# Attention heads of two transformer blocks taken in pairs, two gates by tanh instead of sigmoid, and one weight unit moved

## The reference, cut to what matters

```
first block:   ada = silu(c) @ w_ada + b_ada          # six vectors of 1024: shift, scale, gate, twice
               h = modulate(rmsnorm(x), ...);  proj = h @ w_in
               o_gla  = rmsnorm(gated linear attention, 4 heads) * silu(gr)
               o_moba = causal softmax attention, 8 heads of 64, with a relative bias
               x += gate_a * (concat(o_gla, o_moba) @ w_out)
               h = modulate(rmsnorm(x), shift_m, scale_m)
               x += gate_m * (relu(h @ w_ff1)**2 @ w_ff2)          # d_ff = 4096
second block:  z = rmsnorm(x) @ w_in_2
               attention of 8 heads of 64: softmax(q k^T / 8 + log(number of patterns that see the pair)) v
               conv = silu(layer_norm(depthwise convolution of 31 taps of a * sigmoid(b)))
               x += concat(attn, conv) @ w_out_2
               16 experts of width 2816, each takes its 32 best tokens: (silu(t w1) * (t w3)) w2
```

## Time and profile before

| | us |
|---|---|
| median of three timed runs | 1866.55 |
| the profiled execution | 1867.52 |
| its span, first to last instruction | 1865.8 |
| TensorE busy, share of the span | 1368.2, 73% |
| VectorE busy | 271.8, 15% |
| ScalarE busy | 230.3, 12% |
| GpSimd busy | 39.3, 2% |
| mean granted TensorE clock | 0.832 of full speed |
| data read from memory | 647.38 MB, 348 GB/s over the span |

### The profile page before, as it was taken

One profiled execution on the slowest core, in us unless ns is written; L12 is line 12 of the kernel. 1 busy time (PEld: TensorE's weight loads), 2 busy tenths in 40 slices (PEclk: granted clock), 3 DMA queues, 4 the chain that ended last, 5 costly groups with the idle time before them and its releaser, 6 DMA issues.

```text
span 1865.8 us, 24015 instructions
## 1 busy us (share of the span) xinstructions
PE 1368.2 (73%) x10574; PEld 839.2 (45%) x10574; DVE 271.8 (15%) x557; ACT 230.3 (12%) x530; POOL 39.3 (2%) x64
## 2 busy tenths in 40 slices
PE   7997999999999686565656747666665766756665
PEld 4584888888656343232323414233231423423232
DVE  1213200005952201010000100001010000100001
ACT  1333222002133110000100000010000100000010
POOL 0000000002020000000000000000000000000000
PEclk9998999999989777787777777777787787777778
DMA  9736343432442999999999999999999999999998
GB/s 348 304 125 270 154 172 125 181 137 110 183 187 92 380 438 432 432 433 424 440 430 433 429 431 429 429 435 433 432 433 431 435 433 433 433 433 433 422 441 342
DMA packets 48248, 649.02 MB, mean 348 GB/s; under 512 B 3832, under 2 KB 6336, under 8 KB 31056
## 3 DMA queue, kind: packets, MB, share of 16 engines
q1 hardware_dynamic: 45152, 643.90, 81.7%
q10 hardware_dynamic: 2848, 3.55, 0.6%
q0 software_dynamic: 208, 1.00, 0.1%
HBM read 647.38 MB, written 1.06 MB: 348 GB/s over the span
## 4 chain that ended last, share of the span: by engine, by line
DMA 58%; PE 12%; DVE 1%; issue 1%; ACT 0%; POOL 0%; SPq 0%; DVEq 0%; PEldq 0%; ACTq 0%; POOLq 0%
DMA ring<-in_w 58%; PE ps L1185 11%; DVE small L1083 0%; DVE arena L1133 0%; DVE arena L1135 0%; DVE arena L1079 0%; DVE xT L1177 0%; ACT L701 0%; ACT L689 0%; POOL arena L461 0%; DVE arena L1152 0%; ACT arena L689 0%; SPq L371 0%; DVE arena L1057 0%; ACT arena L704 0%
## 5 line engine op out<-in xcount | busy, mean ns | idle before, releaser
L1185 PE MATMUL ps<-ring,table 128*32 128x352 f32 x4032 | 433.9, 600 | 270.6 <-DMA ring<-in_w 270.6
L1185 PEld LDWEIGHTS ps<-ring,table 128*32 128x32 f32 x4032 | 154.0, 140 | 535.3 <-issue 339.6
L1185 PE MATMUL ps<-ring,arena 128*32 128x256 f32 (+1 forms) x2818 | 196.5, 437 | 149.3 <-DMA ring<-in_w 149.0
L1185 PEld LDWEIGHTS ps<-ring,arena 128*32 128x32 f32 (+1 forms) x2818 | 102.8, 125 | 245.1 <-issue 147.3
L1185 PE MATMUL ps<-hT,ring 128*128 128x256 f32 (+1 forms) x880 | 194.9, 382 | 2.9 <-PE ps L1185 1.4
L1185 PE MATMUL ps<-arena,ring 128*128 128x256 f32 (+1 forms) x800 | 177.5, 382 | 4.0 <-POOL arena L461 2.4
L1185 PEld LDWEIGHTS ps<-hT,ring 128*128 128x128 f32 (+1 forms) x880 | 164.9, 189 | 31.7 <-issue 6.8
L1185 PEld LDWEIGHTS ps<-arena,ring 128*128 128x128 f32 x800 | 152.5, 191 | 27.2 <-issue 3.7
L1185 PE MATMUL ps<-arena 32*128 32x256 f32 (+10 forms) x532 | 97.6, 383 | 27.0 <-DVE xT L1177 12.2
L1185 PEld LDWEIGHTS ps<-arena,hT 128*128 128x128 f32 x512 | 106.7, 322 | 9.3 <-issue 9.3
L1185 PE MATMUL ps<-arena,hT 128*128 (+1 forms) x512 | 108.9, 393 | 1.8 <-DVEq L1161 1.8
(11 more groups left out here) (226 smaller groups left out, 535.2 us busy)
## 6 DMA issues: line engine op xcount, KB each, us to landing
ring<-in_w SPq DMA_DIRECT2D x76, 5632.0 KB, 32.9
ring<-in_w SPq DMA_DIRECT2D x19, 2816.0 KB, 28.3
ring<-in_w SPq DMA_DIRECT2D x35, 1408.0 KB, 31.1
ring<-in_w_ff SPq DMA_DIRECT2D x8, 4096.0 KB, 14.1
ring<-in_w_ada SPq DMA_DIRECT2D x6, 4096.0 KB, 15.4
ring<-in_w_in SPq DMA_DIRECT2D x3, 4096.0 KB, 13.9
ring<-in_w_in SPq DMA_DIRECT2D x5, 2048.0 KB, 18.9
ring<-in_w_out SPq DMA_DIRECT2D x2, 4096.0 KB, 13.4
```

Of the source, the lines that this page charges most:

```text
L1185: return pe.matmul(o, w, x, start=first, stop=last)
```

## The change

Nothing that is computed changes, but for the form of two gates. The head loops run over four pairs of heads in place of ten single steps. In a pair p TensorE issues: turn head 2p, scores of heads 2p + 2 and 2p + 3 (their matmuls alternately, one on rows 0 to 63, one on rows 64 to 127), turn head 2p + 1, the fillers of the pair, and the values of both heads (alternately on columns 0 to 63 and 64 to 127). VectorE and ScalarE take the same operations in pairs. The values now end with a wait of TensorE for their own completion in the first block as well (`pv_set`). `ada3` goes ahead of the pairs, `ada4` into pair 2; `ada5` leaves the loop and is computed after the first unit of ff1, and its weights are fetched after ff1_0's. Both gates are u * (1 + tanh(u)): gr is taken with scale 0.5, the layer norm's gain and bias are halved (`halfgb`, two small VectorE operations), and ScalarE does Tanh and then an Identity with bias 1.0. In the second block it does so for two halves of 512 columns, and GpSimd's products wait for one half each.

```diff
-UNITS = ([... "ada3", "win_r", "ada4", "wout", "ada5"]
-         + [f"ff1_{u}" for u in range(4)] + ...
+UNITS = ([... "ada3", "win_r", "ada4", "wout", "ff1_0", "ada5"]
+         + [f"ff1_{u}" for u in range(1, 4)] + ...
-FREED = ["ada1", "ada0", "win_a", "win_v", "ada2", "win_c", "win_r", "ada3", "ada4", "ada5", "wout"] + UNITS[11:]
+FREED = ["ada1", "ada0", "win_a", "win_v", "ada2", "win_c", "ada3", "win_r", "ada4"] + UNITS[9:]
-FILLER = {0: "gr1", 1: "gr2", 2: "gr3", 3: "ada3", 4: "at3", 5: "ada4", 6: "at4", 7: "ada5", 8: "at5"}
+FILLER = {0: ("gr1",), 1: ("at3", "gr2", "gr3"), 2: ("ada4",), 3: ("at4",)}
 ...
 # GpSimd, second block's gate
+            pool.wait_ge(s["gg2_set"], 2)
             for m in range(CT):
-                nc.gpsimd.tensor_scalar(..., vcol("conv_ln_g_2", m), vcol("conv_ln_b_2", m), ALU.mult, ALU.add)
+                nc.gpsimd.tensor_scalar(..., halfgb[:, m:m + 1], halfgb[:, 4 + m:5 + m], ALU.mult, ALU.add)
             pool.wait_ge(s["cln_set"], CT)
-            pool.wait_ge(s["csg_set"], 1)
             for m in (0, 2):
+                pool.wait_ge(s["csg_set"], 1 + m // 2)
                 nc.gpsimd.tensor_tensor(mix2[:, 4 + m:6 + m, :], mix2[:, 4 + m:6 + m, :], csq[:, m:m + 2, :], ALU.mult)
 ...
 # ScalarE, first block
+            for p in range(MH // 2):
+                for i in (2 * p, 2 * p + 1):
+                    (wait for max_set, two Exp with their sums)
+                for j in (2 * p, 2 * p + 1):
+                    if p >= 1:
+                        wait_filled(act, f"pv{p - 1}")
+                    take(f"pT{j}", pTb[:, j % 2, :], bk(f"pT{j}")[:, 0:384], s["pT_set"], j + 1)
+                for h in ((1,), (2, 3), (), ())[p]:
+                    gr_take(h)
+                if p == 1:
+                    link(A(flat(sgr), flat(gr), ACT.Tanh))
+                    A(flat(sgr), flat(sgr), ACT.Identity, bias=1.0).then_inc(s["sgr_set"], 1)
 ...
 # ScalarE, second block: the same pairs (takes of uT wait for pw_set 2p), and
+                if p == 0:
+                    for m in (0, 2):
+                        act.wait_ge(s["cln_set"], m + 2)
+                        link(A(flat(csq[:, m:m + 2, :]), flat(mix2[:, 4 + m:6 + m, :]), ACT.Tanh))
+                        A(flat(csq[:, m:m + 2, :]), flat(csq[:, m:m + 2, :]), ACT.Identity, bias=1.0)
 ...
 # VectorE, first block
+            for p in range(MH // 2):
+                scored(2 * p); scored(2 * p + 1); divided(2 * p); divided(2 * p + 1)
+                if p == 0:
+                    ada_rows(3); gla_root(0)
+                if p == 1:
+                    headed(0); ada_cols(3); gla_root(1); gla_root(2)
+                if p == 2:
+                    headed(1); gla_root(3); gla_scaled(0); gla_scaled(1)
+                if p == 3:
+                    ada_rows(4); gla_scaled(2); gla_scaled(3)
+                    for h in range(GH):
+                        gla_gated(h)
+                    headed(2); headed(3); ada_cols(4)
 ...
 # VectorE, second block
+            for p in range(MH // 2):
+                scored(2 * p)
+                scored(2 * p + 1)
+                if p == 0:
                     dve.wait_ge(s["cvar_set"], 1)
                     V.reciprocal(lnr, lnr).then_inc(s["crec_set"], 1)
+                divided(2 * p)
+                divided(2 * p + 1)
+                if p >= 1:
+                    headed(p - 1)
+            headed(MH // 2 - 1)
 ...
 # TensorE, first block
+            scores(0)
+            fill("ada3")
+            for p in range(MH // 2):
+                turned(2 * p)
+                if p + 1 < MH // 2:
+                    scores(p + 1)
+                turned(2 * p + 1)
+                for name in FILLER[p]:
+                    fill(name)
+                weighted(p)
 ...
 # TensorE, ff1
+                    if u == 1 and m == 0:
+                        ada_turn(5)
+                if u == 0:
+                    ada_part(5)
 ...
 # TensorE, second block
+            scores(0)
+            finish("v1", v1_part(7, 8))
+            pe.wait_ge(s["xr_set"], 2)
+            z_start(0)
+            z_start(1)
+            for p in range(MH // 2):
+                turned(2 * p)
+                if p + 1 < MH // 2:
+                    scores(p + 1)
+                turned(2 * p + 1)
+                if p == 0:
+                    z_start(2)
+                    z_start(3)
+                for c in ((), (4,), (5, 6), (7,))[p]:
+                    z_conv(c)
+                weighted(p)
+            for c in range(CT):
+                z_heads(c)
```

More of the change, by code:

```diff
@@ L41 @@
 AR = 14536
-UNITS = (["ada1", "win_a", "ada0", "win_v", "ada2", "win_c", "ada3", "win_r", "ada4", "wout", "ada5"]
-         + [f"ff1_{u}" for u in range(4)] + [f"ff2_{u}" for u in range(4)]
+UNITS = (["ada1", "win_a", "ada0", "win_v", "ada2", "win_c", "ada3", "win_r", "ada4", "wout", "ff1_0", "ada5"]
+         + [f"ff1_{u}" for u in range(1, 4)] + [f"ff2_{u}" for u in range(4)]
          + ["conv", "qk", "v", "wo2"])
 UNIT = {name: i for i, name in enumerate(UNITS)}
-FREED = ["ada1", "ada0", "win_a", "win_v", "ada2", "win_c", "win_r", "ada3", "ada4", "ada5", "wout"] + UNITS[11:]
+FREED = ["ada1", "ada0", "win_a", "win_v", "ada2", "win_c", "ada3", "win_r", "ada4"] + UNITS[9:]
 ADA = [1, 0, 2, 3, 4, 5]
-FILLER = {0: "gr1", 1: "gr2", 2: "gr3", 3: "ada3", 4: "at3", 5: "ada4", 6: "at4", 7: "ada5", 8: "at5"}
+FILLER = {0: ("gr1",), 1: ("at3", "gr2", "gr3"), 2: ("ada4",), 3: ("at4",)}
 assert [UNIT[name] % 3 for name in ("v", "wo2", "qk")] == [0, 1, 2]
@@ L73, in bank_plan @@
     order += ["klT", "att0", "att1", "kv0", "kv1", "gr0", "o0", "o1", "gs0", "gs1"]
[L74 to L82 removed]
+    order += ["sc0", "sc1", "ada3"]
+    for p in range(MH // 2):
+        order += [f"pT{2 * p}"] + [f"sc{j}" for j in (2 * p + 2, 2 * p + 3) if j < MH] + [f"pT{2 * p + 1}"]
+        order += [*FILLER[p], f"pv{p}"]
+    order += ["n_mlp"] + [f"y{m}" for m in range(C)] + [f"f{m}" for m in range(C)] + ["ada5", "f8", "at5"]
+    order += [f"f{m}" for m in range(C + 1, FF // P)]
     held["n_mlp"] = {f"y{m}" for m in range(C)} | {"f0"}
@@ L249, in build @@
         csq = ar(0, 1024, m=CT)
+        halfgb = small[:, 88:96]
         stash = ar(0, 4 * SLOT)
@@ L578, in gr_take @@
             def gr_take(h):
[L579 removed]
+                take(f"gr{h}", gr[:, h, :], bk(f"gr{h}")[:, 0:S], s["gr_set"], h + 1, scale=0.5)
             gr_take(0)
@@ new lines, in scored @@
+            def scored(i):
+                b, buf = i % 2, tcb[i % 4]
+                wait_filled(dve, f"tc{i}")
+                if i >= 4:
+                    wait_filled(dve, f"uT{i - 4}")
+                if i >= 1:
+                    dve.wait_ge(s["max_set"], i + MH)
+                for st in range(ST):
+                    half = slice(st * S, (st + 1) * S)
+                    ins = V.tensor_tensor_reduce(buf[:, half], bk(f"tc{i}")[:, half], lnc[:, half], HD ** -0.5,
+                                                 2 * NEG, ALU.add, ALU.max, mx[:, st:st + 1])
+                link(ins)
+                empty(dve, f"tc{i}")
+                V.tensor_scalar(mneg[:, 2 * b:2 * b + 2], mx, -1.0, None, ALU.mult).then_inc(s["max_set"], 1)
@@ new lines, in divided @@
+            def divided(j):
+                b = j % 2
+                dve.wait_ge(s["exp_set"], 2 * j + 2 + 2 * MH)
+                link(V.reciprocal(rinv[:, 2 * b:2 * b + 2], rsum[:, 2 * b:2 * b + 2]))
+                if j >= 2:
+                    wait_filled(dve, f"uT{j - 2}")
+                for st in range(ST):
+                    V.tensor_scalar(diag[:, b, st * P:(st + 1) * P], ident[:, :], rinv[:, 2 * b + st:2 * b + st + 1],
+                                    None, ALU.mult).then_inc(s["diag_set"], 1)
@@ new lines, in scores @@
+            def scores(p):
+                for j in (2 * p, 2 * p + 1):
+                    wait_emptied(pe, f"sc{j}")
+                for k in range(2):
+                    for j in (2 * p, 2 * p + 1):
+                        hp = 64 * (j % 2)
+                        if k == 0:
+                            mm(bk(f"sc{j}")[:, 0:P], mq[hp:hp + HD, p, 0:P], mk[hp:hp + HD, p, 0:P], True, True)
+                        else:
+                            inc_filled(mm(bk(f"sc{j}")[:, P:P + S], mq[hp:hp + HD, p, P:2 * P], mk[hp:hp + HD, p, :],
+                                          True, True), f"sc{j}")
@@ new lines, in fill @@
+            def fill(name):
+                if name.startswith("gr"):
+                    proj(name, w_r, int(name[2]) * P, hT, last=(name == "gr3"))
+                elif name.startswith("ada"):
+                    ada_part(int(name[3]))
+                else:
+                    ada_turn(int(name[2]))
+            scores(0)
+            fill("ada3")
+            for p in range(MH // 2):
+                turned(2 * p)
[5 more added lines that the diff above has]
+                weighted(p)
@@ new lines, in scores @@
+            def scores(p):
```

(9 more changed lines are left out.)

304 lines of the change are left out of this document (115 added, 189 removed).

## The result

| | before | after |
|---|---|---|
| median, us (lowest to highest, executions) | 1866.50 (1865.74 to 1866.79, 4) | 1853.71 (1853.18 to 1853.93, 4) |
| ratio to before, 95% interval | 1 | 0.9930 (0.9914 to 0.9946) |
| profiled execution / span, us | 1867.52 / 1865.8 | 1853.62 / 1851.9 |
| first head loop, us | 54.94 | 38.86 |
| between the head loops, us | 348.12 | 352.25 |

The account below looks back on a forecast made before the run. The experts' transfers bound the kernel, so savings before them pass to the end: 10.3 us (14.5 - 4.2) plus 3.5 gives 13.8, from 1867.52 to 1853.7, median 1852.7 us; range 1847.5 to 1859, the forecast's own 1850 to 1856.

Parts of the forecast that it names:

- The bound: Experts' stage, 1251.6 us and bound by transfers, stays unchanged; whatever is won or lost before it passes to the end.
- The first loop: First head loop: y0 at 169.6 against 184.08, 14.5 us less, with 1.5 us taken for lost clock.
- The stops of 1.4 and 4.6: First head loop: TensorE waits 1.4 us before turn 2 and 4.6 us before turn 4.
- ada5 behind ff1_0: Between the loops: ada5 is moved, not removed, costing 4.2 us on TensorE there; order costs 0, up to 2.
- The second loop: Second head loop: stops of 3.6 and 2.2 us, 5.1 us less at full clock, 3.5 us after lost clock.
- The clock term: Second head loop: one more stretch at the lower clock, costing 1.6 us, between 0 and 3.4.
- Tanh without a load: ScalarE's gates in both loops: tanh needs no table load after exp, cost taken as 0 of up to 2.56 a loop.
- Rival (a): ScalarE, both loops: tanh and then exp load tables, costing 5.1 us in all; 1857.8 us, chance 0.13.
- Rival (b): Both loops: the softmax chain bounds every pair, costing 9.3 us; 1862.0 us, chance 0.10.
- (c): Both loops: clock stays at 2.4 GHz and GpSimd doesn't hold up VectorE; 18 us gained, 1848.5, chance 0.15.
- (d): Both loops: more pauses keep the clock at 1.2 GHz, 40 us lost with both low, about 1885; chance 0.04.
- the median of the runs lies 1.0 lower: Last step of the sum: from 1853.7 us for the profiled execution to a median of 1852.7 us.

Follow-up runs that it names:

- the version with the gates late: Against the change, ScalarE's takes of gr and both gates put behind the next pair's exponentials: 1846.02 us, ratio 0.9891.
- the late reciprocal: VectorE's layer-norm reciprocal in the second block behind the divisions of heads 0 and 1: on the change 1855.62 us, with gates behind exponentials 1840.88 us.

## Why the prediction was right, and where it was not

**The bound.** Right: 1251.50 us for the experts against 1251.63, so every us before them reached the end.

**The first loop.** I had y0 at 168.1 at full clock and 169.6 with the lost clock. It came at 167.99 in the first profiled execution and at 168.90 in the other (whose loop began at 127.57, so that it is 2.5 us longer). The stops of 1.4 and 4.6 measured 1.56 and 4.43, and their causes are shown: ScalarE's order by the version that takes them away, GpSimd's product by the one that holds it back. That 168.1 was met in the first execution is in part luck, for the clock did fall. TensorE's work from turn 4 to the end of values 2 took 8.20 us, with 3.41 of them at the lower clock, and the same work takes 6.65 in the version with the gates late: about 1.5 us, as I had taken. They were paid, too: turn 6 came at 164.93, 0.30 behind TensorE's own work, and not at 164.2, bound by VectorE. Two other steps made up for them. Turn 4 came at 156.42, 0.9 earlier than I had it, and from turn 6 to y0 it was 3.1 us instead of 3.9. VectorE's last product ended at 167.18, so at full clock y0 would have come at most 0.8 earlier.

**ada5 behind ff1_0.** 4.2 us expected; the stage between the loops grew by 4.13, and no unit was waited for. But I booked the stop of 5.47 as what the move removes. The runs say otherwise: with pairs and the early ada3 the stop is gone with ada5 still in the loop. By SyncE's rows it is the early ada3 that lets the queue go on; it was never run without the pairs. The move brought 5.7 us to the kernel before, and to the paired one nothing that the medians show (1851.91 with ada5 in the loop, 1853.71 and 1853.13 without).

**The second loop.** Turn 0 at 540.1 on the old scale: 520.24 to 528.11 is 7.87 us, and 532.20 + 7.87 = 540.07. The first stop was 3.43 for 3.6. In VectorE's rows the division ahead of turn 0 takes 2.29 us beside GpSimd's product and 0.64 for the next head, so the product can account for nearly all of the 1.8 by which that stop shrinks when the reciprocal, and the product with it, comes later. The second stop was 2.18 for 2.2. Without its two lowered stretches (half of 3.42 each) the loop would be 57.6 us, and I had 57.8. The clock term was mis-sized: 3.4 us, not 1.6. TensorE's work shrank as summed: 57.77 us with 3.41 at the lower clock before, 49.93 at full clock in the version with the gates late, so 6.1 us for the 5.8 of the prediction.

**Tanh without a load.** Right, no load stands at L607. The Trainium skill, "ScalarE: Activation LUTs", section "Table sets: the hidden batching unit", puts exp and tanh in one set, and the trace agrees. Rival (a)'s price of 5.1 let the loads through in full. With the sigmoids put back, the stops grew by 0.5 and 1.3 us, and the rest of their 4.3 was the clock; that 4.3 is near 5.1 is chance.

**Rival (b).** The softmax chain did not bind every pair. Where ScalarE had nothing else ahead of the exponentials, TensorE didn't wait for it: 0.34 before turn 4 of the second block. The Trainium skill's rule on copies out of PSUM ("TensorEngine Tiling (Array Packing)", section "PSUM Bottleneck") bears on a small part of it: of what stood ahead of exponential 4, the copy of gr3 is 0.38 us and the gate 2.1. The stops came from the order, and in another order they were gone.

**Rivals (c) and (d).** Neither came. GpSimd held VectorE up, and in the first execution the clock fell once in the first loop and twice in the second, but the granted clock was 0.96 and 0.94, not 0.50. The price of (d) is wrong by its own rule: the 81 us of work at full clock would take twice as long at the lower level, so some 80 us more and not 40.

**The sum.** In the profiled executions: 16.1 from the first loop, less 4.1 between the loops, 2.0 from the second, 0.2 lost on the router, 0.1 won in the experts: 13.9, for 13.8 expected. Two errors made up for each other: the first loop's steps came 1.7 us shorter than I had them, and the second loop's clock term was 1.8 too small.

**The step that failed** is the last: "the median of the runs lies 1.0 lower". I took the distance of one execution from the median as a property of the kernel. It was the spread: executions of the change reach from 1852.88 to 1855.23, and the profiled one lay 0.09 from its median. So 1853.71 came out where 1852.7 was forecast, within the range and within my own range of 1850 to 1856.

**What I had not worked out** is how the parts share the gain. From the medians: the pairs alone 10.9, the move of ada5 alone 5.7, tanh alone 0; pairs with tanh 14.5, pairs with ada5 moved 8.3, all three 12.8 to 13.2. They don't add: two of the parts take away the same stop, and tanh counts only where ScalarE is what TensorE waits for. Differences of 1 to 3 us among these hold the clock's share too, as the sigmoids' 4.3 did.

## What to carry to other kernels

Two heads on different halves of the array need only stand next to each other; then look at what stands ahead of the next exponentials in ScalarE's queue, since moving the gates behind them gave 7.7 us here (the clock's part in it included), and the change itself 13. Before a stop is booked to the part that moves its transfer away, ask which other part gives that transfer more time. An offset between one profiled execution and the median is spread until a second profile shows it again.

## What the runs showed of the hardware that I had not expected

**VectorE beside GpSimd.** While GpSimd runs a product of two inputs (2.34 us), a VectorE TENSOR_SCALAR of 128x128 takes 1.40 us instead of 0.29. It ends as the product does (156.11 and 156.02), and in the earlier trace rows likewise (538.63 and 538.61): VectorE seems to wait for the product's end rather than to run slowly beside it. With the gates late it is the first scaling (2.25 us instead of some 0.5). This was the price that I took from the earlier trace rows.

**Where the clock falls differs between executions.** The stretches at 1.2 GHz were between 3.4 us and, from the router into the first expert, 20.5 us long. In the change's first execution they followed the stops of 4.43, 3.43 and 2.18 us but not that of 1.56; in its second there was one at 141.2 too, behind that stop, and only one in the second loop. Each costs about half its length where TensorE is busy, so the late reciprocal, whose stops cost 0.6 us on one kernel and gained 1.0 on the other, came out 2.5 us slower on the one and 5.1 us faster on the other, and in the profiled executions most of that is the clock. Which stop draws one is left open.
